# Modulation vectors of a two-layer diffusion step: raw fp32 weight blocks as the stationary operand, and the twelve vectors made at four places

## The reference, cut to what matters

```
mod_ctx = silu(c_ctx) @ w_mod[l] + b_mod[l]      # w_mod[l]: 1024 x 6144, fp32
mod_lat = silu(c)     @ w_mod[l] + b_mod[l]
shift1, scale1, gate1, shift2, scale2, gate2 = split(mod, 6)
h = rms_norm(x, g_norm1) * (1 + scale1) + shift1
x = x + gate1 * token_mixing(h)                  # 4 mixers, gates, output projection
h = rms_norm(x, g_norm2) * (1 + scale2) + shift2
x = x + gate2 * expert_choice_ffn(h)             # router, top-k per expert, 16 SwiGLU experts
```

## Time and profile before

| | |
|---|---|
| median of 3 runs | 2959.8 us (2955.29 to 2965.03) |
| the profiled execution | 2957.3 us, span 2955.4 us |
| granted TensorE clock, mean | 0.963 |
| PE busy | 2677.4 us, 91% |
| VectorE, ScalarE busy | 1970.5 and 1587.2 us |
| bytes from HBM | 566.73 MB |

### The profile page before, as it was taken

The page is one execution under the profiler, slowest core; times in us unless marked ns, Lnnn a source line. Parts: engine busy times, 40 slices in busy tenths (PEclk is TensorE's granted clock), DMA queues, the critical chain, the costliest instruction groups (busy, mean ns, idle before and its releaser), DMA issues.

```text
span 2955.4 us, 40730 instructions
## 1 busy us (share of the span) xinstructions
PE 2677.4 (91%) x13616; PEld 1913.4 (65%) x13616; DVE 1970.5 (67%) x3045; ACT 1587.2 (54%) x2302; POOL 469.1 (16%) x363
## 2 busy tenths in 40 slices
PE   7889999999995899999979999998999499999994
PEld 1267777777774566666648777787777366666662
DVE  7873366444436799999966346643434699999994
ACT  6743444333323677777753444433422287777773
POOL 1103000221210122121211100031122112211211
PEclk9989999999997899999999999999999699999997
DMA  9932111121333799999982211121124399999994
GB/s 360 380 123 57 39 40 43 43 67 41 119 136 121 278 384 377 380 374 388 376 291 78 74 33 37 36 79 36 59 101 163 109 369 379 385 372 377 386 379 167
DMA packets 191304, 593.75 MB, mean 201 GB/s; under 512 B 23752, under 2 KB 33798, under 8 KB 191174
## 3 DMA queue, kind: packets, MB, share of 16 engines
q1 hardware_dynamic: 171638, 527.66, 48.2%
q0 software_dynamic: 19536, 64.38, 7.4%
HBM read 566.73 MB, written 25.23 MB: 200 GB/s over the span
## 4 chain that ended last, share of the span: by engine, by line
PE 78%; DVE 8%; issue 5%; ACT 5%; DMA 3%; SPq 0%; POOL 0%; ACTq 0%; DVEq 0%; POOLq 0%
PE bank L465 21%; PE bank L467 20%; PE bank L466 20%; PE bank L841 4%; PE bank L813 4%; PE bank L831 2%; DVE low L1346 2%; DMA ring<-in_w_mod 2%; ACT high L1039 2%; PE bank L953 1%; DVE st L1591 1%; PE bank L990 1%; DVE sigr L1521 1%; DVE att L1426 1%; PE bank L624 1%
## 5 line engine op out<-in xcount | busy, mean ns | idle before, releaser
L1039 ACT ACTIVATE high<-ring 128x1024 fp32r<-128x1024 f32 (+1 forms) x1008 | 1056.3, 1052 | 416.1 <-PE bank L467 368.6
L1732 DVE TENSOR_TENSOR low<-ring,high 128x1024 fp32r<-128x1024 f32 x736 | 880.0, 1220 | 73.3 <-ACT high L1039 70.9
L465 PE MATMUL bank<-high,hT_high 128*128 128x512 f32 (+2 forms) x1280 | 521.1, 407 | 25.5 <-ACT sigr L1108 13.5
L466 PE MATMUL bank<-low,hT_high 128*128 128x512 f32 (+2 forms) x1280 | 486.0, 380 | 0.0
L467 PE MATMUL bank<-high,hT_low 128*128 128x512 f32 (+2 forms) x1280 | 484.1, 378 | 0.0
L465 PE MATMUL bank<-high,xeT_high 128*80 128x512 f32 x1056 | 419.0, 397 | 5.6 <-issue 3.5
L467 PE MATMUL bank<-high,xeT_low 128*80 128x512 f32 x1056 | 416.6, 394 | 0.0
L466 PE MATMUL bank<-low,xeT_high 128*80 128x512 f32 x1056 | 416.4, 394 | 0.0
L1346 DVE TENSOR_TENSOR low<-ring,high 128x1024 fp32r<-128x1024 f32 (+2 forms) x272 | 322.4, 1208 | 132.2 <-ACT high L1039 131.3
L1209 ACT ACTIVATE att<-bank,st 128x640 f32<-128x640 f32 (+3 forms) x200 | 136.5, 683 | 348.6 <-DVE st L1596 254.0
L465 PEld LDWEIGHTS bank<-high,hT_high 128*128 128x128 f32 x1280 | 243.4, 190 | 79.1 <-ACT sigr L1108 18.1
(11 more groups left out here) (240 smaller groups left out, 3280.2 us busy)
## 6 DMA issues: line engine op xcount, KB each, us to landing
ring<-in_w_e_gate SPq DMA_DIRECT2D x256, 512.0 KB, 6.0
ring<-in_w_e_up SPq DMA_DIRECT2D x256, 512.0 KB, 6.9
ring<-in_w_e_down SPq DMA_DIRECT2D x256, 512.0 KB, 6.2
ring<-in_w_mod SPq DMA_DIRECT2D x96, 512.0 KB, 6.4
ring<-in_w_gate SPq DMA_DIRECT2D x64, 512.0 KB, 3.8
ring<-in_w_in SPq DMA_DIRECT2D x24, 512.0 KB, 4.4
ring<-in_w_branch SPq DMA_DIRECT2D x16, 512.0 KB, 4.1
ring<-in_w_out SPq DMA_DIRECT2D x16, 512.0 KB, 4.6
```

The costliest lines, as they stand in the source:

```text
L465: nc.tensor.matmul(out, lhs[0], rhs_high, start=start, stop=False)
L466: nc.tensor.matmul(out, lhs[0], rhs_low, start=False, stop=False)
L1039: A(high[:, HSLOT[g], :, 0:w], ring[:, SLOT[g], :, 0:w], ACT.Copy).then_inc(high_done, 1)
L1732: V.tensor_tensor(low[:, SLOT[ahead], :, :], ring[:, SLOT[ahead], :, :], high[:, HSLOT[ahead], :, :].bitcast(F32), ALU.subtract).then_inc( ...
```

## The change

- `w_mod` chunks no longer go through the ring and are not split. They are loaded as fp32 into twelve 4 KB-per-partition slots of their own, laid over buffers that are free at the time (seven in `U`, four in `M`, one in `sigr`).
- A 128 x 128 block of a chunk is now the stationary operand, in full fp32, and what moves is the fp32 pair of silu columns, read 32 times over by a stride of nothing: 64 columns. A vector is 64 such matmuls into one PSUM bank, opened by one matmul that adds the bias (512 columns). The vector stands as 8 columns for each condition; `mod_turn` turns it to rows and POOL stores those as before, in two DMAs. Where it is a scale, POOL adds 1 and multiplies by the gain first.
- The twelve vectors are made in this order and at these places: at the very start scale1, shift1 and gate1 of layer 0; between the tiles of norm 1 of layer 0 its scale2 and shift2; in the router gap of layer 0 scale1 and shift1 of layer 1, gate2 of layer 0 and gate1 of layer 1; in the layer turn scale2 of layer 1, and between the tiles of norm 1 of layer 1 its shift2; in the router gap of layer 1 its gate2.
- x tiles 1 to 4, constants and the small weights are issued later at the start; `gate2` is loaded in the gap behind the first gathers, and VectorE waits for it ahead of the expert loop.

The diff, cut to its core:

```diff
+VECTORS = [(0, 1), (0, 0), (0, 2), (0, 4), (0, 3),
+           (1, 1), (1, 0), (0, 5), (1, 2),
+           (1, 4), (1, 3), (1, 5)]
+MOD_BANK = [4, 6, 4, 6, 4, 0, 5, 0, 5, 6, 4, 5]
+GAINS = [n for n, (_, s) in enumerate(VECTORS) if s in (1, 4)]
+REP = NW // KD // 2
+MOD_PLACE = {"front": range(0, 5), ("gap", 0): range(5, 9), "turn": range(9, 11), ("gap", 1): range(11, 12)}
...
 def _(sp):
+            def mod_fill(c):
+                n, k = divmod(c, KD)
+                l, s = VECTORS[n]
+                if MOD_FREE[c] is not None:
+                    sp.wait_ge(mod_used, MOD_FREE[c])
+                sp.dma_start(mod_slot[MOD_SLOT[c]], w_mod[l, k * P:(k + 1) * P, s * D:(s + 1) * D]).then_inc(mod_full[MOD_SLOT[c]], 16)
+            for n in (0, 1):
+                mod_fills(n)
...
+                        if l == 0 and i == "D":
+                            mod_fills(MOD_NO[0, 2])
+                            small_loads()
+                            mod_fills(MOD_NO[0, 4])
+                        if l == 0 and i == "Aq":
+                            mod_fills(MOD_NO[0, 3])
+                        if l and i == "D":
+                            sp.wait_ge(ring_used, chunk_no(l, 0))
+                            for k in range(3, 2 * KD):
+                                mod_fill(MOD_NO[1, 4] * KD + k)
...
                         if i is None and SLOT[g + k] == 13:
+                            sp.wait_ge(x_new, T * (l + 1))
+                            for j in range(2):
+                                mod_fill(MOD_PLACE["gap", l][0] * KD + j)
+                            sp.wait_ge(xn_ready, T * (2 * l + 2))
+                            for j in range(2, 6):
+                                mod_fill(MOD_PLACE["gap", l][0] * KD + j)
...
                 matrix(w_e_up, 0, g0 + CH_GATE0)
+                for j in range(6, KD * len(MOD_PLACE["gap", l])):
+                    mod_fill(MOD_PLACE["gap", l][0] * KD + j)
...
 def _(pe):
+            def mod_chunk(c):
...
+                if k == 0:
+                    if n >= 2:
+                        pe.wait_ge(mod_rows, n - 1)
...
+                    mm(bank(MOD_BANK[n]).rearrange("p (b r) -> p b r", b=KD), b_rows[:, :], own, start=True, stop=False, skip_group_check=True)
+                pe.wait_ge(mod_full[MOD_SLOT[c]], 16 * MOD_FILLS[c])
+                for b in range(KD):
+                    ins = mm(cols[:, b, :, :], mod_slot[MOD_SLOT[c]][:, b * P:(b + 1) * P], csf[:, k:k + 1, :].broadcast_to([P, REP, 2]),
+                             start=False, stop=(k == KD - 1), skip_group_check=True)
+                ins.then_inc(mod_used, 1)
+            def mod_turn(n):
+                pe.wait_ge(mod_cols, n + 1)
+                tr(bank(MOD_BANK[n], P, 2 * P)[0:2 * KD, :], mcol[:, :], ident[:, :]).then_inc(mod_turned, 1)
+            for n in range(3):
+                mod_chunks(n, 0, KD)
+                mod_turn(n)
...
+                woven = [MOD_NO[0, 4], MOD_NO[0, 3]] if l == 0 else [MOD_NO[1, 3]]
                 if l:
+                    mod_chunks(MOD_NO[1, 4], 0, KD)
+                    mod_turn(MOD_NO[1, 4])
...
                     if m < T - 1:
                         norm_turn(q1, m + 1, 0)
+                        share = 2 * len(woven)
+                        for i in range(m * share, (m + 1) * share):
+                            mod_chunk(woven[i // KD] * KD + i % KD)
                     pe.wait_ge(norm_low, 2 * (T * q1 + m + 1))
                     dense_tile(("W", "D"), m)
...
                 turn_logits(T - 1).then_inc(lg_full, 1)
+                n0 = MOD_PLACE["gap", l][0]
+                mod_chunks(n0, 0, 6)
                 pe.wait_ge(aff_ready, l + 1)
...
+                mod_chunks(n0, 6, KD)
+                mod_turn(n0)
+                for n in MOD_PLACE["gap", l][1:3]:
+                    mod_chunks(n, 0, KD)
+                    mod_turn(n)
                 pe.wait_ge(top_ready, l + 1)
...
+                for n in MOD_PLACE["gap", l][3:]:
+                    mod_chunks(n, 0, KD)
+                    mod_turn(n)
                 pe.wait_ge(topT_ready, l + 1)
                 rows_turn(0, 16 * (NE // 2 * l + 1))
...
 def _(act):   # mod_cols_out: bank -> mcol; mod_rows_out: the turned rows -> modsum
 def _(pool):
+                    x_load(0)
+                    pool.wait_ge(gcol_ready, 1)
+                    mod_gain_cols(0)
+                    mod_store(0)
+                    for m in range(1, T):
+                        x_load(m)
+                    mod_store(1)
+                    pool.wait_ge(mod_out, 32 * 2)
+                    for g in (1, 0):
+                        mod_in(q1, g)
...
                 gather(1, NE * l + 2)
-                pool.wait_ge(gate2_in, 32 * (l + 1))
+                mod_store(MOD_NO[l, 5])
+                pool.wait_ge(mod_out, 32 * (MOD_NO[l, 5] + 1))
```

More of the change, by code:

```diff
@@ L38 @@
 SLOT_E = [8, 9, 10, 11, 12, 0, 1, 2, 3, 4, 5, 6, 7, 13, 14, 15]
-N_MOD = 6 * D // NW
-CH_MOD = NQ * N_MOD * L
 N_GATE = 8
@@ L247, with plan_mods @@
 LOOP_FILLS = 2 * CH_EXP // RING_E
+VECTORS = [(0, 1), (0, 0), (0, 2), (0, 4), (0, 3),
+           (1, 1), (1, 0), (0, 5), (1, 2),
+           (1, 4), (1, 3), (1, 5)]
+MOD_NO = {v: n for n, v in enumerate(VECTORS)}
+MOD_BANK = [4, 6, 4, 6, 4, 0, 5, 0, 5, 6, 4, 5]
+GAINS = [n for n, (_, s) in enumerate(VECTORS) if s in (1, 4)]
+REP = NW // KD // 2
+MOD_PLACE = {"front": range(0, 5), ("gap", 0): range(5, 9), "turn": range(9, 11), ("gap", 1): range(11, 12)}
+MOD_SLOTS = ["U0", "U1", "U2", "U3", "U4", "U5", "U6", "S0", "M0", "M1", "M2", "M3"]
+def plan_mods():
+    slot, fills, free = [], [], []
+    count, last = {}, {}
+    order = {"front": ["U0", "U1", "U2", "U3", "U4", "U5", "U6"], "turn": ["U0", "U1", "U2", "U3", "U4", "U5", "U6"]}
+    for place, vectors in MOD_PLACE.items():
+        last = {}
+        names = order.get(place, ["U5", "U6", "M0", "M1", "M2", "M3"])
+        for i in range(KD * len(vectors)):
+            if place == "turn":
+                name = "S0" if i == 2 else names[(i - (i > 2)) % len(names)]
+            else:
+                name = names[i % len(names)]
+            count[name] = count.get(name, 0) + 1
+            slot.append(name)
+            fills.append(count[name])
+            free.append(None if name not in last else last[name] + 1)
+            last[name] = len(slot) - 1
+    return slot, fills, free
+MOD_SLOT, MOD_FILLS, MOD_FREE = plan_mods()
 def hybrid_step(nc, x_prompt, x_sample, cache_diff_k, cache_diff_v, cache_na_k, cache_na_v, cache_swa_k,
@@ L362, in hybrid_step @@
         csf = sb("csf", [P, KD, 2])
[L363 to L367, removed]
+        b_rows = sb("b_rows", [L * 6 * KD, P])
+        modsum = sb("modsum", [2 * KD, P])
+        mcol = sb("mcol", [P, 2 * KD])
+        gcol = sb("gcol", [P, 2 * L * KD])
+        g_rows = att[0:2 * L * KD, 7168:7168 + P]
+        mod_slot = {f"U{i}": U[:, i * D:(i + 1) * D] for i in range(7)}
+        mod_slot["S0"] = sigr[:, 1024:2048]
+        for i in range(4):
+            mod_slot[f"M{i}"] = M[:, i * D:(i + 1) * D]
         st = sb("st", [P, 160])
@@ L529, in _ @@
                     sp.wait_ge(on_ready, T * l)
+                    sp.wait_ge(xe_tr, 2 * NE * l)
+                    sp.wait_ge(top_ready, l)
+                    for k in range(3):
+                        mod_fill(MOD_NO[1, 4] * KD + k)
                 row = lambda a: a.rearrange("(a n) -> a n", a=1)
@@ L540, in _ @@
                 ]
-                for dst, src in small:
-                    sp.dma_start(dst, src).then_inc(small_in, 16)
-                for dst, src in [
+                caches = [
                     (c_ka, cache_diff_k[0, l].rearrange("t h n -> t (h n)")),
@@ L552, in _, with small_loads @@
                     (c_kpe[:, 64:96], cache_mla_kpe[0, l]),
-                ]:
-                    sp.dma_start(dst, src).then_inc(small_in, 16)
+                ]
+                def small_loads():
+                    for dst, src in small + caches:
+                        sp.dma_start(dst, src).then_inc(small_in, 16)
+                if l:
+                    small_loads()
                 n = 0
@@ L625, in turn4 @@
                 ins.then_inc(done, 1)
[L629 to L660, removed]
-                if q:
-                    mod_tail(q - 1)
@@ L666, in _, with mod_chunks @@
+            def mod_chunks(n, a, b):
+                for k in range(a, b):
+                    mod_chunk(n * KD + k)
+            def mod_turn(n):
[4 more added lines that the diff above has]
+                mod_turn(n)
             for l in range(L):
@@ L743, in qm @@
                     ins.then_inc(qm_full, 1)
+                after_woven = woven[-1] + 1
                 norm_turn(q1, 0, 0)
@@ L1138, in _ @@
                     norm_highs(q1, m)
-                    if l == 0 and m == 0:
-                        for b in range(2):
-                            act.wait_ge(mod_out[b], 16 * 3 * L)
```

(8 more changed lines are left out.)

193 lines of the change are left out of this document (97 added, 96 removed).

## The result

The changed kernel is slower. Its 11 runs have a median of 3012.89 us (2968.34 to 3552.36) against 2960.7 us for the kernel before. The medians of all runs are 1.8% apart. The times fall in groups: five at 2968 to 2983 us with a mean granted clock of 0.978 to 0.980, five at 3013 to 3025 us with 0.963 to 0.965, and one far out at 3552 us with 0.742; the kernel before has such a run too, at 4863 us, so that one is not laid to the change. The profiled execution (3013.24 us, span 3011.4) is of the upper group; a second profile of the same kernel, `e0_again` (2982.93 us, span 2981.1), is of the lower one. Both are read here.

A forecast was written before the change was run, and what follows sets the result against it. PE, busy 91% of the span, was taken as the bound, the start as waiting for bytes. 2957.3 - 110.7 + 29.3 + 24 + 18 + 4 = 2921.9, forecast 2923 us; 8-in-10 range 2897 to 2957.

The forecast's parts named there:

- Vector 0: 14.5, plus 3 for a start at the low clock: Start: first vector begins at 9.0 us, takes 14.5 plus 3 us for the low clock, and ends at 26.5.
- 1.70 us a chunk: PE price of a raw chunk at full clock: 16 matmul records, 106 ns from one start to the next.
- The term -110.7 us: Start: first norm turn at 62 us instead of 172.75; bounds 57 to 68.
- signs that the prediction named for being wrong: Clock row at 0.5 in start or gap, starts over 134 ns apart, or PE idle over 30 us in new turns.
- The aside on shorter landings: Start: at 2.0 us fixed per DMA, store and read land some 5 us sooner; vector 2 binds, sum 2 lower.
- The clock falls in the raw stretches: Rival: 1.2 GHz, 3.4 us a chunk; 3073 us, or some 3030 if only unwoven stretches fall; chance 0.14.
- the new stretches have no such pauses: Argument against the clock falling: raw stretches lack the 1.5 us pauses beside which the earlier trace's clock was down.
- Norm 1, layer 0: Two vectors woven between norm 1's tiles in layer 0 are pure addition: +29.3 us; 3 more if their other steps weren't covered.
- Router gap, layer 0: Four vectors between layer 0's logits and first expert matmul: the row turn starts 25.8 us late, +24 after warm-clock savings.
- Layer turn: Between layers, chunk loads share wires with x tiles and gains: 4 us late, between 0 and 9; with woven vector 10, +18.
- Router gap, layer 1: Six chunks ahead of L940 take 11.1 us against 6.88 idle, the rest hides in top-k: +4 us.
- The sum: Total of all stage terms from 2957.3 us: 2921.9, forecast as 2923.

The follow-up runs named there:

- e3: Changed kernel with four dense fp32 matmuls of 512 columns on the identity ahead of vector 0; median 2964.03 us, ratio 0.9992 to the kernel before.
- e1: Changed kernel with 128 moving columns, two PSUM banks and a second bias matmul in the nine vectors not woven into norm 1; median 2948.7 us, ratio 0.9950.
- after: First profiled execution of the changed kernel, nothing edited; 3013.24 us, span 3011.4.
- e6: e5 with dense dummy matmuls: three behind layer 0's first norm turn, four and two around vector 9's turn, vector 9 moved behind two PE waits; median 2940.07 us.
- e4: e3 with the scale vector's turn put two chunks into the next vector, at the start and in the first gap; median 2950.75 us, ratio 0.9961.
- e7: e1's wide vectors with e4's turns, e5's late fills, e6's dummies, no matmuls ahead of the start, a gain-column wait behind vector 0; median 2933.24 us, ratio 0.9906.
- e5: e4 with SP, in the layer turn, waiting for a read x tile before loading vector 10's chunks; median 2952.66 us, ratio 0.9970.
- e8: e6 with vector 2's loads issued ahead of constants and "D" weights; median 2935.12 us, ratio 0.9915.
- e2: Changed kernel with only the two real columns moving per block instead of 64; median 3066.03 us, ratio 1.0358.

## Why the prediction was wrong, point by point

**The step that failed** is the start's "Vector 0: 14.5, plus 3 for a start at the low clock", and with it the use of 1.70 us a chunk for the vectors behind it. The 106 ns of the earlier trace rows were nearly right for the high clock (111 ns from start to start over 128 records, so a vector is 15.3 us where 14.5 was said) and the load-bound form was right too: with 2, 64 or 128 columns the price is the same at one level. Wrong was that the clock would rise by itself, as it did in the expert stretch of the earlier trace rows; there 512 columns move per load. It never rose there: 214 ns for all 384 records, and the first turn at 96.9 where 62 was said. The term -110.7 us measured -75.9. Two of the signs that the prediction named for being wrong came, starts over 134 ns apart and a low clock in the gap (0.57). e3 shows the cause, with the same blocks at 14.40 us a vector once dense work had raised the clock, and e1 (62.0) shows that the start can be had as forecast.

**Terms of the start that were off without effect.** The stores landed after 2.3 us (median of 24), not 5.1. The aside on shorter landings is added wrongly: its own figure for a transfer, taken twice in place of 5.1 and 6.9, gives 8 us sooner, not 5. Vector 2 ends last in either case.

**The rival was named, and priced at one event.** "The clock falls in the raw stretches" had a chance of 0.14 and times of 3073 us everywhere or 3030 in the unwoven stretches. What happened is split: at the start always, in the first gap in some executions, in vector 9 of the turn never, and in the first woven chunks of norm 1, of either layer, in some executions, where PE came out of a wait. Its first turn at 100 was close to 96.9 and its gap of +83 above the +68 measured. I had read the earlier trace rows rightly (pauses drop the clock), and then said that "the new stretches have no such pauses", though the same prediction put 2.2 us into each scale vector's turn. That turn held a pause of 1.05 us, and at it the clock fell in `after` and in e3. With the pause covered or with 128 columns none of 39 runs lay in an upper group (25 of them have 64 columns and the covered pause); with it and 64 columns (the changed kernel and e3) 11 of 31 did.

**Norm 1, layer 0:** +29.3 predicted, +33.3 and +41.4 measured; e6's 62.0 us for the stage, dummies and all, is 2.3 over my estimate of 59.7, so weaving was rightly "pure addition" at the high clock. The rest is the cold first stretch.

**Router gap, layer 0:** +24 predicted, +25.7 at the high clock in e0_again, +24.4 in e4. L1025 stands 11.8 us after the last logits turn where the working gave 11.3. Right in mechanism and size, without the chance of a fall; with it +68.

**Layer turn:** +4 predicted for the shared wires, +8.0 measured, inside the bounds of 0 to 9: 4.5 of it is the scatter, which the working had left out of what shares the wires with the 13 chunks, and 3.6 the reads. The landings above show what it left out: in the kernel before, too, the scatters take 8.7 us (median of all 32, most of them beside the experts' weight loads), and 5.1 at the end of each layer, where no loads stand beside them. The woven vector of layer 1 cost 15.1 to 15.3 where 14 was said.

**Router gap, layer 1:** +4 predicted, +4.2 measured. `gate2` and what else is late behind it cost at most the 1.6 to 1.9 us by which the last stage grew.

**The sum** with the measured terms, e0_again: 2957.3 - 76.0 + 41.4 + 3.8 + 25.7 + 8.1 + 15.3 + 1.3 + 4.2 + 1.9 = 2983.0 against its 2982.93. Had the clock held, the other terms were good to 10 us: e7, which holds it, ran at 2933 where the forecast said 2923, and 3.8 of that is its longer gap with the doubled bias matmuls (69.0 against e4's 65.2).

**What stays open:** why the same pause of 1.05 us drops the clock in one execution and not in the next; why two runs of the changed kernel went to 3552 and 5050 us and one of the kernel before to 4863 (none is profiled); what of e1's gain is the columns' and what the second bias matmuls'; and how many loads beside it the scatter bears, since it took 10.4 us in e5 with only five chunks left ahead of it. A kernel with all loads behind the scatter was not tried.

## What to carry to other kernels

A price read from a short burst holds at the clock of that burst: before it is multiplied, ask what raises the clock where the new work stands, and price the stretch at both levels. Here blocks with 64 moving columns kept the clock that they found, 214 ns a record for 90 us or 112 ns, and a pause of 1 us could cost the high one. What helped was dense work ahead of them, no pause between them, and 128 columns, which cost nothing under the load but a second bias matmul. When a wait is taken away at the head of a kernel, read the in-order queue of the next engine first, since the wait may only move there, as in e8.

## What the runs showed of the hardware

- Records of an fp32 128 x 128 block start 212 to 213 ns apart at the low clock with 2, 64 or 128 moving columns (e2, `after`, the first twelve of e1), and 109, 111 and 112 ns apart at the high one. Up to 128 columns the load sets the price.
- Three vectors of 27.4 us with 64 columns a load, 1.04 and 0.29 us of pause between them, did not raise TensorE's clock from 1.2 GHz; with 128 columns and a second bias matmul it rose 2.6 us into the first vector (15.68 us against 14.45 for the next). At the high level both ran a whole vector without losing it; with 2 columns it fell even in stretches woven between dense matmuls.
- The clock fell at a pause of 1.05 us between 64-column stretches in two of the profiles and not in a third; a wait of 3.03 us in a 128-column stretch did not drop it.
- The clock column said 1.00 for the first 97 us of `after`, while records there took twice their time at the high level.
- A scatter of one expert's rows had its follower wait 10.3 us from its issue beside thirteen loads of 512 KB, and 5.8 us without them; it landed after 9.6 and 5.1 us, and after 5.2 us at the end of `after`, where no loads stand beside it.
